# Six of the 48 modulation weight chunks summed over k tiles on VectorE, with 12 matmuls over partitions in place of 48 over everything

## The reference

```python
silu_c = jax.nn.silu(c)
silu_cc = jax.nn.silu(c_ctx)
for i in range(DEPTH):
    mod_l = (silu_c @ ada_w[i] + ada_b[i])[:, None, :]
    mod_c = (silu_cc @ ada_w[i] + ada_b[i])[None, None, :]
    sh1_l, sc1_l, g1_l, sh2_l, sc2_l, g2_l = jnp.split(mod_l, N_MOD, axis=-1)
    ...
    a_l = ada_norm(h, norm_mix[i], sh1_l, sc1_l)
    a_c = ada_norm(hc, norm_mix[i], sh1_c, sc1_c)
    ...            # attention, residual scaled by g1, then a feed-forward block with sh2, sc2, g2
```

## Time and profile before

| | before |
|---|---|
| median of 3 runs | 1522.08 us |
| lowest, highest | 1519.97, 1522.39 us |
| profiled execution | 1518.34 us, span 1517.1 us |
| PE busy | 1500.7 us, 99% |
| DVE busy | 944.2 us, 62% |
| ACT busy | 713.7 us, 47% |
| mean granted TensorE clock | 0.999 |

### The profile page before, as it was taken

One profiled execution on the slowest core, in us unless ns is written; L12 is line 12 of the kernel. 1 busy time (PEld: TensorE's weight loads), 2 busy tenths in 40 slices (PEclk: granted clock), 3 DMA queues, 4 the chain that ended last, 5 costly groups with the idle time before them and its releaser, 6 DMA issues.

```text
span 1517.1 us, 21399 instructions
## 1 busy us (share of the span) xinstructions
PE 1500.7 (99%) x8911; PEld 1251.2 (82%) x8911; DVE 944.2 (62%) x1245; ACT 713.7 (47%) x1007; POOL 77.9 (5%) x104
## 2 busy tenths in 40 slices
PE   7999999999999999999999999999999999999998
PEld 5777767778888888879778888899888888988887
DVE  6532585553424332467977666679789856779973
ACT  5422585342213222346765455545656546566553
POOL 0210141000000000000010000024000000000000
PEclk9999999999999999999999999999999999999999
DMA  9766425452532232464255555656565554565652
GB/s 360 240 194 216 128 48 171 169 188 87 191 111 83 85 110 91 149 206 131 65 169 192 179 183 184 206 177 219 177 196 183 193 196 154 180 208 168 196 192 84
DMA packets 243248, 252.42 MB, mean 166 GB/s; under 512 B 17757, under 2 KB 234176, under 8 KB 243152
## 3 DMA queue, kind: packets, MB, share of 16 engines
q1 hardware_dynamic: 241600, 248.53, 50.3%
q0 software_dynamic: 944, 1.87, 0.3%
q10 hardware_dynamic: 608, 0.66, 0.1%
HBM read 248.94 MB, written 1.05 MB: 165 GB/s over the span
## 4 chain that ended last, share of the span: by engine, by line
PE 86%; DVE 7%; ACT 5%; issue 1%; DMA 0%; SPq 0%; DVEq 0%; ACTq 0%
PE psum L415 83%; DVE wl L401 4%; ACT wh L394 3%; PE psum L1011 3%; ACT scr L1052 1%; DMA vtok<-in_ctx 0%; DVE scr L1916 0%; ACT scr L1883 0%; PE psum L982 0%; DVE scr L1914 0%; DVE scr L1908 0%; DVE hT L2148 0%; DVE scr L593 0%; PE psum L580 0%; DVE x L603 0%
## 5 line engine op out<-in xcount | busy, mean ns | idle before, releaser
L401 DVE TENSOR_TENSOR wl<-raw,wh 128x2048 fp32r<-128x2048 f32 (+1 forms) x183 | 413.6, 2262 | 222.4 <-ACT wh L394 222.2
L394 ACT ACTIVATE wh<-raw 128x2048 fp32r<-128x2048 f32 (+1 forms) x183 | 344.3, 1883 | 292.3 <-PE psum L415 291.1
L415 PE MATMUL psum<-x,wh 128*128 128x512 f32 (+1 forms) x1520 | 461.3, 363 | 0.5 <-DVE wl L401 0.4
L415 PE MATMUL psum<-x,wl 128*128 128x256 f32 x1312 | 367.8, 280 | 0.0
L415 PEld LDWEIGHTS psum<-x,wh 128*128 128x128 f32 x1520 | 271.6, 188 | 48.6 <-issue 2.2
L415 PEld LDWEIGHTS psum<-x,wl 128*128 128x128 f32 x1312 | 248.4, 189 | 0.0
L415 PE MATMUL psum<-xh,wh 128*128 128x512 f32 (+1 forms) x624 | 239.1, 383 | 0.3 <-DVE xl L762 0.3
L415 PE MATMUL psum<-xl,wh 128*128 128x512 f32 (+1 forms) x624 | 236.2, 379 | 0.0
L415 PE MATMUL psum<-xh,wl 128*128 128x512 f32 (+1 forms) x624 | 236.2, 379 | 0.0
L415 PEld LDWEIGHTS psum<-xh,wh 128*128 128x128 f32 x624 | 117.4, 188 | 29.0 <-DVE xl L603 4.3
L415 PEld LDWEIGHTS psum<-xh,wl 128*128 128x128 f32 x624 | 117.4, 188 | 22.1
(11 more groups left out here) (287 smaller groups left out, 1990.6 us busy)
## 6 DMA issues: line engine op xcount, KB each, us to landing
raw<-in_ffn_w_in SPq DMA_DIRECT2D x44, 1024.0 KB, 4.9
pre<-in_ada_w SPq DMA_DIRECT2D x26, 1024.0 KB, 9.7
raw<-in_ada_w SPq DMA_DIRECT2D x22, 1024.0 KB, 5.9
raw<-in_w_ffn_gate SPq DMA_DIRECT2D x22, 1024.0 KB, 5.2
raw<-in_w_ffn_up SPq DMA_DIRECT2D x22, 1024.0 KB, 5.1
raw<-in_w_ffn_down SPq DMA_DIRECT2D x19, 1024.0 KB, 5.0
raw<-in_ffn_w_out SPq DMA_DIRECT2D x16, 1024.0 KB, 5.0
raw<-in_na_w_qkv SPq DMA_DIRECT2D x10, 1024.0 KB, 5.8
```

The lines of the kernel that those rows point to most:

```text
L394: act.e.activation(wh[:, c % NSPL, 0:z], raw[:, p % NRAW, 0:z], ACT.Copy).then_inc(W.hi, 1)
L401: dve.e.tensor_tensor(wl[:, c % NSPL, 0:z], raw[:, p % NRAW, 0:z], wh[:, c % NSPL, 0:z].bitcast(F32), ALU.subtract).then_inc(W.lo, 1)
L415: return pe.e.matmul(o, l, r, start=start, stop=stop, skip_group_check=shared)
```

## The change

Chunks 14, 15, 16, 17, 30 and 31 leave the `raw` slots and get places in the arena (`pre40`, `pre56`, `pre96` twice, `pre94`, `pre102`). DVE multiplies each k tile of such a chunk by the scalar of its partition out of `cz` and adds up the eight, for c and for c_ctx: 16 instructions of 256 columns for each chunk, eight in one turn and eight in the next (`ada_half_dve`, turns 2 to 9 of qkv0 and 2 to 5 of ffn0). Each of them waits on the semaphore `Y.step` for the last but one before it. PE then adds the sums over the partitions with two matmuls for each chunk, with a stationary operand of zeros and one column of ones (`ada_sum_pe`), into the same bank and partition groups as before. SP waits on `Y.step` before it loads chunk 17 into the place of chunk 16, ACT and DVE wait on it before they write `kh0` and `v0` over the places.

```diff
-        after = {2: [8, 9], 4: [10, 11], 6: [12, 13], 8: [14, 15], 9: [16, 17], 10: [18, 19]}
+        after = {2: [8], 4: [9, 10], 6: [11, 12], 8: [13], 10: [18, 19]}
+        SUMMED = (14, 15, 16, 17, 30, 31)
...
-        after[first_ffn0 + 1] = [30, 31]
...
+                elif (kind, x) == ("w", 4):
+                    sp.wait_ge(A.used, 8)
+                    sp.wait_ge(N.xl, 2 * KT)
+                    load_staged((14,))
+                elif (kind, x) == ("w", 6):
+                    load_staged((15, 16))
...
+                elif (kind, x) == ("w", 11):
+                    sp.wait_ge(Y.step, 48)
+                    load_staged((17,))
+                elif (kind, x) == ("w", first_ffn0 + 3):
+                    sp.wait_ge(A.used, 30)
+                    load_staged((30, 31))
...
+        def ada_half_dve(p, half):
+
+            a = SUMMED[p]
+            w, sums = view(pre[staged[a]], 0, ada_src(a)), ada_sums(a)
+            dve.wait_ge(s_pre[lane[a][0]], lane[a][1])
+            for k in range(4 * half, 4 * half + 4):
+                for s in range(2):
+                    to, by, n = sums[:, s * T:s * T + T], cz[:, k, 30 + s:31 + s], 16 * p + 2 * k + s
+                    if k == 0:
+                        dve.e.tensor_scalar(to, w[:, k, :], by, None, ALU.mult).then_inc(Y.step, 1)
+                    else:
+                        dve.wait_ge(Y.step, n - 1)
+                        dve.e.scalar_tensor_tensor(to, w[:, k, :], by, to, ALU.mult, ALU.add).then_inc(Y.step, 1)
+
+        def ada_sum_pe(ps):
+            for p in ps:
+                a = SUMMED[p]
+                b, q = place[a]
+                pe.wait_ge(Y.step, 16 * p + 16)
+                for s in range(2):
+                    j, c = 2 * (p % 2) + s, 23 - (2 * q + s)
+                    last = mm(ada_bank(b)[32 * j:32 * j + 32, 0:256], oz[:, c:c + 32], ada_sums(a)[:, s * T:s * T + T], False,
+                              a >= 30)
+                last.then_inc(A.used, 1)
...
                 if t == 3:
                     ada_pe(c)
+                    if (g, piece) == (1, 0):
+                        ada_sum_pe(range(4))
...
+            if g == 0:
+                e.wait_ge(Y.step, 64)
             if g == 0 and t < 3:
                 e.wait_ge(X.tile, KT + t + 1)
...
                 if i < 8:
                     act.wait_ge(W.used, c + 1)
+                    if i == 6:
+                        act.wait_ge(Y.step, 16)
...
                 if i:
                     split_for(split_lo, c)
+                if 2 <= i < 10:
+                    ada_half_dve(i // 2 - 1, i % 2)
...
-                    if c < first_qkv1 - 2:
-                        ada_pe(c)
-                    if c == first_ffn0 + 2:
+                    if c == first_ffn0 + 5:
+                        ada_sum_pe((4, 5))
+                    if c == first_ffn0 + 6:
                         ada_fold(NEXT)
...
-            if g == 2:
+            if 2 <= g < 6:
+                ada_half_dve(3 + g // 2, g % 2)
+            elif g == 6:
                 ada_copy(NEXT)
-            elif g == 3:
+            elif g == 7:
                 ada_add(NEXT)
                 coefs_dve(1, 0)
```

More of the change, by code:

```diff
@@ L110, in program @@
         gain = sb("gain1", [P, 2])
+        oz = sb("oz", [P, 54])
         rq = sb("rq", [P, 32])
@@ L138, in program @@
         vrow = at(48, "vrow", [P, 3, P])
-        pre = {kib: at(kib, f"pre{kib}", [P, 1, 2048]) for kib in (0, 8, 16, 24, 32, 40, 54, 62, 70, 72, 78, 86, 88, 96)}
+        pre = {kib: at(kib, f"pre{kib}", [P, 1, 2048]) for kib in (0, 8, 16, 24, 32, 40, 54, 56, 62, 70, 72, 78, 86, 88, 94, 96, 102)}
         hn = at(32, "hn", [P, KT, TT])
@@ L143, in program @@
         xh1, xl1 = at(0, "xh1", [P, KT, TT], F32R), at(16, "xl1", [P, KT, TT], F32R)
+        part2 = at(48, "part2", [P, 2, TT])
         xh2, xl2 = at(54, "xh2", [P, KT, TT], F32R), at(70, "xl2", [P, KT, TT], F32R)
@@ L255, in program @@
         BORDERS = (((20, 21, 22, 23, 24, 25), (26,), (27, 28, 29)), ((32, 33, 34, 35, 36, 37), (38,), (39, 40, 41)), ((42, 43, 44), (45,), (46, 47)))
-        staged = {7: 96, 0: 0, 1: 8, 2: 16, 3: 24, 4: 72, 5: 88, 6: 54, 20: 54, 21: 62, 22: 70, 23: 78, 24: 32, 25: 40, 26: 86,
+        staged = {7: 96, 0: 0, 1: 8, 2: 16, 3: 24, 4: 72, 5: 88, 6: 54, 14: 40, 15: 56, 16: 96, 17: 96, 30: 94, 31: 102, 20: 54, 21: 62, 22: 70, 23: 78, 24: 32, 25: 40, 26: 86,
                   33: 54, 34: 62, 35: 70, 36: 78, 37: 32, 38: 40, 39: 86, 42: 86, 43: 40, 44: 0, 45: 8}
         lane, loaded = {}, [0] * 7
-        for first, last in ((0, 8), (20, 27), (33, 40), (42, 46)):
+        for first, last in ((0, 8), (14, 18), (20, 32), (33, 40), (42, 46)):
             for i, a in enumerate(sorted(x for x in staged if first <= x < last)):
@@ L479, in program, with ada_sums @@
         A = semaphores(nc, "ada", "used copied folded mod")
+        Y = semaphores(nc, "adasum", "step")
+        def ada_sums(a):
+            return scr[:, a - 14, :] if a < 20 else part2[:, a - 30, :]
+        def ada_half_dve(p, half):
[20 more added lines that the diff above has]
+                last.then_inc(A.used, 1)
         def ada_bank(b):
@@ L732, in setup_dve @@
             dve.e.memset(rstd[:, :], 0.0).then_inc(C.dve, 1)
+            dve.e.memset(oz[:, 0:23], 0.0)
+            dve.e.memset(oz[:, 24:54], 0.0)
+            dve.e.memset(oz[:, 23:24], 1.0)
             dve.wait_ge(L.cst, 16)
```

## The result

| | before | after |
|---|---|---|
| median of 22 runs each | 1520.94 us | 1523.11 us |
| lowest, highest | 1518.56, 1522.54 us | 1522.21, 1524.39 us |
| ratio, 95% interval | | 1.0016 (1.0010 to 1.0022) |
| profiled execution | 1518.34 us, span 1517.1 us | 1523.2 us, span 1522.0 us |

A forecast was written before the change was run, and what follows sets the result against it. PE was taken to bound both touched stretches, with DVE's work and the new waits hidden. Profiled 1518.34 us less 4.2 us of PE records gave 1514.1, scaled to timed runs 1517.9 us, 0.28% less; range 1514.3 to 1521.6.

The forecast's parts named there:

- a shift of the whole program that no row points to: Whole program: the remainder left after the forecast and its four-way list of outcomes, chance 0.03, with no size given.
- PE's records: PE, qkv0 and ffn0: 96 modulation records go, 24 come, each 0.058 us (bounds 0 and 0.382): 4.2 us less.
- Rule on weight loads: PE: the skill's rule that weight loads overlap running matmuls only with different row groups; 32 loads would need 3.5 us.
- rival 4: PE's records: each costs its own 109 ns load, so 7.8 us go and the time is 1514.3 us; chance 0.05.
- DVE's half: DVE, qkv0 and ffn0: eight instructions take 3.2 us, at most 4.8, and fit in idle gaps.
- a half above 6 us: DVE: a half chunk's eight instructions lasting over 6 us was listed as a sign that the prediction is wrong.
- The tightest place, the value copy: ACT, qkv0 turn 9: the copy waits for all sums, done by 139.9; PE's turn 10 starts at 142.7, 2.8 us room.
- Rival 3: Value copy in qkv0 gates PE's turn 10 because DVE's instructions are slow: 1524.8 us at 1.6 us each; chance 0.07.
- The small constants: L868 loads: landed by 55.7 us; PE reads them 0.9 us earlier than 61.57, with 4.9 us of room.
- rival 2: One wait, likeliest L868's loads (1521.3 us), or short sums at 0.2 us a record pays back part; chance 0.17.
- SP's new waits: SP, qkv0 and ffn0: weights queued behind waits or added chunks still arrive in time; nothing lost.
- The prediction's last warning: Behind 170 us: it fails too if earlier stages win 4.2 us and a later one, loads or splits unmoved, gives it back.

The follow-up runs named there:

- gap_before: The kernel before the change plus an unused tensor of 216 bytes a partition where `oz` stands in the changed one: 1527.16 us, ratio 1.0041.
- oz_last: The changed kernel with `oz` allocated behind all other tensors, so the large ones keep their addresses from before the change: 1515.46 us, ratio 0.9961 to before.
- before_again: The kernel before the change, unchanged, profiled a second time: 1523.36 us.

## Why the prediction was wrong

**The step that failed** is one that the sum doesn't contain. It prices what the instructions of the change do and costs the tensor `oz`, with all that it pushes, at nothing. The text has "a shift of the whole program that no row points to" at 0.03, and no row did: no row shows an address. What moves could be read from the allocation list; what the move costs could not be read from any row (the earlier trace rows show a full queue, but from 43 us on, and at one placement only). The runs showed it: the empty tensor of gap_before, which prices this term alone, costs 0.41% in the timed runs, more than the 0.28% that the sum promised. The sum between after and oz_last, the same program in other places (8.45 us at the end):

- 3.1 us at the start, there in every misplaced kernel, and shown by shifts of 32, 64, 128 and 224 bytes: this is caused by the places;
- 3.0 us at 1087 to 1243 us and 2.1 us behind 1338 us, in every execution with 224 bytes: linked to the places, the first also seen without any shift, mechanism open;
- 1.5 us of clock, which comes without the change too, and 1.5 us back between 711 and 995 us, where after went mostly at the fast pace and oz_last mostly at the slow one;
- 0.2 us between 995 and 1087.

**The terms that were in the sum held.**

- *PE's records, 4.2 us.* Visits lost with four chunks: -2.83 + 0.13 = 2.7 us at 154.6 in oz_last (forecast: four chunks and eight short sums at 0.058, (64 - 16) x 0.058 = 2.8). At the end -3.64, at 687 us -3.92. The sums on PE cost what old records cost; neither bound (0 or 0.382 us each) was near. In the timed runs oz_last is even 0.39% better. The surplus over 0.26% may be what the clock and the late pace add to some runs of before (before_again is 5.0 us above before); no run shows it.
- *Rule on weight loads (rival 4).* 16 loads of 110 ns one after the other would be 1.76 us; all 16 started within 0.5 us. The trace disagrees again.
- *DVE's half, 3.2 us, upper bound 4.8.* Eleven halves of twelve take 3.0 or 3.25 us, as forecast, and one was far outside. The 0.1 us for a semaphore round in the upper bound has no row behind it, and none of the eleven needed it. Two turns of after:

```profile
80.72 2.46 DVE L511 SCALAR_TENSOR_TENSOR scr<-pre,rstd,scr 128x256 f32<-128x256 f32 x6
86.57 1.29 DVE L1008 SCALAR_TENSOR_TENSOR kl<-psum,kh 128x512 fp32r<-128x512 f32 x2 [3.40 <-ACT kh L978]
88.86 2.29 DVE L415 TENSOR_TENSOR wl<-raw,wh 128x2048 fp32r<-128x2048 f32 x1 [1.00 <-ACT wh L408]
91.07 5.64 DVE L511 SCALAR_TENSOR_TENSOR scr<-pre,rstd,scr 128x256 f32<-128x256 f32 x8
```

  Six steps in 2.46 us are 0.41 us each, as in the earlier trace rows. The half at 91.07 takes 5.64 us, and in oz_last 7.14. It costs nothing all the same: DVE takes the turn's result at 99.54, 8.5 us behind the half's start, and idles for 2.83 us ahead of it (1.33 us in oz_last). The prediction named a half above 6 us as a sign of failure; in oz_last it was none.
- *The tightest place, the value copy.* ACT in oz_last:

```profile
139.31 1.09 ACT L983 ACTIVATE v<-psum 128x512 f32<-128x512 f32 x2 [5.53 <-DVE scr L511]
142.75 1.92 ACT L408 ACTIVATE wh<-raw 128x2048 fp32r<-128x2048 f32 x1 [2.35 <-PE psum L429]
```

  The copy waits 5.53 us for DVE's sums and starts at 139.31 (forecast: 139.3); PE ends turn 9 at about 142.7 (forecast: 142.7) and doesn't wait. Rival 3 didn't come.
- *The small constants (rival 2).* PE reads them at 60.58 in oz_last, 0.99 earlier than the earlier trace rows (forecast: 0.9), without a wait. *SP's new waits* delayed nothing that PE reads.

The prediction's last warning, that a later stage might give the gain back, came true in after behind 687 us, but not through loads or splits: from 687 us on PE waits for neither in after.

**The best version** is oz_last: 1515.46 us, with the change's instructions untouched.

## What to carry to other kernels

A new tensor is part of a change even if it holds 216 bytes: see what stands behind it in the allocation, and put it behind everything large, or measure the kernel before with an empty tensor of the same size, which separates the places from the instructions in one run. An expected gain of 0.3% can be judged only against the same places, and a stretch of a trace in which PE has no waits and fewer instructions in the same time points to its clock or its operands' places, not to the schedule. Two single profiles of one kernel can lie 5 us apart through events that come in one execution and not in the next; repeat before explaining. And where a window's granted clock lies between its two levels, ask for shorter windows: they show when it fell, for how long, and what the engine did just ahead.

## What the runs showed of the hardware

- Loads of 1 KB packets with a full queue: 385 GB/s at multiples of 256 bytes in SBUF, 348 at 32, 64, 128 or 224 bytes past one, 359 where only the arena was off, 385 where only `raw` was. Why `raw` alone costs nothing at the start, when its packets are slower later (49.5 against 46.6 ns), is open.
- 512-column matmuls at full clock: 0.227 us each with the places of before, 0.229 with 64 bytes more between arena and the rest, 0.233 with the arena or the split weights moved to 8992.
- Pairs of a 512- and a 256-column matmul: 10.4 or 10.6 us for 30, for long stretches; the slow one filled 1087 to 1243 us in eight of the 14 executions named under the clock.
- The granted clock fell to 1.2 GHz for 3.4 us at the same place of the program in eight of these 14 executions, 0.4 to 1.4 us behind 20 matmuls of 20 and 2 columns (2.1 us) that PE's busy time counts in full. The cost was 1.5 us.
- Two-input DVE steps of 480 ns took 947 ns in the median in a half of after (473 to 960) and 947 to 993 ns in the same half of oz_last, while POOL worked on the attention bias (`bias`). Two of the POOL rows beside the half at 91.07 us in after:

```profile
91.60 0.95 POOL L867 TENSOR_SCALAR_AFFINE_SELECT bias<-bias 64x576 f32<-64x576 f32 x1 [36.58 <-DMA bias<-in_na_rpb]
...
95.41 1.03 POOL L867 TENSOR_SCALAR_AFFINE_SELECT bias<-bias 64x576 f32<-64x576 f32 x1 [0.23 <-DMA bias<-in_na_rpb]
```

  The Trainium skill, SBUF — State Buffer, section "🔬 SBUF: two separate sides", says that a VectorE operation with two inputs in SBUF and a GpSimd operation that reads SBUF shut each other out for the length of an instruction. The traces of both kernels agree, by coincidence in time: steps of about 950 ns beside POOL's instructions of 0.73 to 1.03 us, 480 ns elsewhere. No run moves POOL's work away.
